# Eleven modulation tiles summed by VectorE instead of TensorE, four of them loaded after the experts, and a gather in four column groups

## The chip, the cores and the metric

The kernel runs on one core of a Trainium2 chip. The time is device time in microseconds (us) of one launch; lower is better. Engines are named as in the profile: PE (TensorE), DVE (VectorE), ACT (ScalarE), POOL (GpSimd) and SP, which here only issues DMA.

## What is computed

Two transformer blocks in float32 for 256 latent tokens and 256 context tokens, width 1024. Each layer's shift, scale and gate rows are a product of an activated condition row with a weight w_ada:

```python
mod_lat = jax.nn.silu(c) @ w_ada[l] + b_ada[l]
sh1, sc1, gt1, sh2, sc2, gt2 = jnp.split(mod_lat[:, None, :], 6, axis=-1)
h_lat = modulate(rmsnorm(x_lat, norm_pre_mix[l]), sh1, sc1)      # h * (1 + scale) + shift
y_lat, y_ctx = token_mixer(h_lat, h_ctx, ...)   # differential attention and a two-way recurrence
x_lat = x_lat + gt1 * rmsnorm(y_lat, norm_post_mix[l])
h_lat = modulate(rmsnorm(x_lat, norm_pre_ffn[l]), sh2, sc2)
f_lat = expert_choice_ffn(h_lat, w_router[l], w_gate[l], w_up[l], w_down[l])  # 16 experts, 32 tokens each
x_lat = x_lat + gt2 * rmsnorm(f_lat, norm_post_ffn[l])
# second block, two layers: latent attention (MLA), then a Fourier mixer
sh_l, sc_l, gt_l = ada_params(silu(c_2), w_ada_2[i], b_ada_2[i])
h_lat = h_lat + gt_l * y_lat
return rms_norm(h_lat, final_g)
```

## The kernel before

The program has a section for each engine, in which every instruction and every wait is written out; the order on an engine is the order of the text. Weights come in tiles of 1024 rows by 512 columns (2 MiB) into `ring`, six slots of that size; in the first part only slots 0 to 3 take them, since 4 and 5 serve as scratch. SP issues the loads in the order of the list `stream` and, before each, waits until the last reader of the slot's former tile (`last_reader`) is through. Since SP issues in order, a load that waits holds back all behind it.

The modulation rows are 24 tiles (`("ada", i)`; 0 to 11 of w_ada, 12 to 23 of w_ada_2). `mod_product(i)` (L886) multiplies one on PE: 8 matmuls in four column groups of 32, 16 passes, since a float32 matmul takes two. ACT copies the result (`take_mod`, L1599). For a shift or scale, PE then turns it into columns (`mod_columns`, L897), and DVE adds the bias (L1990); for a gate, a matmul with a broadcast column spreads it over the partitions (`mod_gate`, L905) and DVE adds it to the gate row `G` (`gate_rows`, L2265). Tiles 18 to 21 (`LATE_MODS`) are different: DVE forms their weighted sum (`late_product`, L2484 and L2487), and PE sums over the partitions only.

The work in order of time: the first four tiles, the forget gates, keys, queries and values out of w_in (L867), among them the eight tiles of `COLUMN_MODS` by `mod_step(k)`, which turns one and multiplies the next. Between them run the levels of the recurrence: DVE makes `distance` (L2107, L2108), ACT the decay (L1644), DVE the products (L2119, L2121), PE the matmuls (L1014). Then differential attention over eight pairs of block and head, n = 0 to 7: scores (L1062), max (L2253), exp (L1716), difference (L2281), transposes (L1090), copy (L1721), value product (L867), and at the end of each n the product of one gate tile. Then the output product, the router (L1194) with a top-k on DVE, and the first gather (L1227), which picks 32 tokens for expert 0 in two column groups of 512 columns.

The 16 experts: `gate_up(e)` (L1262), `down(e)` (L1284), `scatter(e)` (L1296). Each has six tiles of 2 MiB, one for each slot. The first two experts' loads are written out, since parts of the second go to free SBUF (`extra`), the rest runs in a loop. A slot is loaded again as soon as its tile is used. After the experts comes the epilogue: the list `late` with the MLA layer's and the Fourier layer's weights, latent attention over eight heads (scores L1458 and L1464, max L2531, transposes L1488), output product, Fourier layer, its output product (L1551).

## Time and profile before

| | us |
|---|---|
| median of 3 runs | 1079.23 |
| lowest and highest | 1076.66, 1079.52 |
| the profiled execution | 1078.76 |
| its span | 1076.9 |

| engine | busy us | share of the span |
|---|---|---|
| PE | 916.0 | 85% |
| DVE | 334.7 | 31% |
| ACT | 204.0 | 19% |
| POOL | 52.9 | 5% |

The DMA queues moved 310.20 MB, 288 GB/s over the span. A line of the timeline has the start in us, the busy time, engine, source line, operation, what it writes and reads, the number of instructions, and in brackets how long the engine was idle before and what ended that. The chain of waits lists, in order of time, the pieces of the chain that ended last.

### The profile page before, as it was taken

The page shows a single profiled execution, that of the slowest core. Times are in us where ns is not written, and L with a number is a line of the kernel's source. Part 1 is how long each engine was busy: PE and PEld are TensorE (multiplying, and loading weights), DVE is VectorE, ACT ScalarE, POOL GpSimd, SP SyncE. Part 2 cuts the span into 40 slices and gives each one's busy share as a digit, 9 for nine tenths or more (in the row PEclk, how much of TensorE's full clock was granted, in tenths as well). Part 3 has the DMA queues.
Part 4 walks back from the last instruction along what each step waited for, and adds up shares of the span by engine and source line. Part 5 has one row for each costly group of instructions (what it writes and reads, how often), then busy time and mean ns, then how long its engine had stood idle before and what let it go on. Part 6 is the DMA issues. An engine that isn't in the chain of part 4 may idle for free.

```text
span 1076.9 us, 11360 instructions
## 1 busy us (share of the span) xinstructions
PE 916.0 (85%) x4458; PEld 471.7 (44%) x4458; DVE 334.7 (31%) x601; ACT 204.0 (19%) x435; POOL 52.9 (5%) x128
## 2 busy tenths in 40 slices
PE   4999999999999888767777766766678999999997
PEld 2666564674544522222222212222223785644773
DVE  2299615473472331111111101001114365412022
ACT  2123322221452210000000000000004114411121
POOL 0200000000200100000000000000001000000000
PEclk9899999999999989998888888888988999999999
DMA  9973633642699799999999999999999397004200
GB/s 348 344 261 125 227 118 117 234 157 78 234 337 395 276 392 428 423 427 428 428 428 428 428 428 428 428 428 428 428 428 399 141 331 294 1 24 152 79 1 39
DMA packets 66343, 310.20 MB, mean 288 GB/s; under 512 B 2833, under 2 KB 5060, under 8 KB 53636
## 3 DMA queue, kind: packets, MB, share of 16 engines
q1 hardware_dynamic: 63844, 301.04, 70.0%
q0 software_dynamic: 2464, 8.68, 2.4%
q8 instruction: 24, 0.39, 0.1%
q14 instruction: 11, 0.09, 0.0%
HBM read 308.66 MB, written 1.05 MB: 288 GB/s over the span
## 4 chain that ended last, share of the span: by engine, by line
PE 60%; DMA 31%; DVE 3%; ACT 2%; issue 2%; SPq 1%; POOL 0%; POOLq 0%; DVEq 0%; ACTq 0%
PE bank L867 36%; DMA ring<-w_up_dram 27%; PE bank L1262 8%; PE bank L886 3%; PE bank L1551 3%; DMA ring<-w_in_dram 2%; DMA ring<-w_down_dram 2%; PE bank L1458 1%; PE bank L1014 1%; PE bank L1284 1%; PE bank L897 1%; PE bank L876 1%; PE bank L1464 1%; ACT junk L1564 1%; PE bank L1488 1%
## 5 line engine op out<-in xcount | busy, mean ns | idle before, releaser
L1262 PE MATMUL bank<-ring,ilat 128*32 128x512 f32 x972 | 147.4, 757 | 103.3 <-DMA ring<-w_up_dram 102.3
L1262 PEld LDWEIGHTS bank<-ring,ilat 128*32 128x32 f32 x972 | 40.6, 134 | 205.2 <-issue 204.0
L2437 DVE TENSOR_TENSOR state<-state,bank 64x512 f32<-64x512 f32 x16 | 11.0, 690 | 303.1 <-ACT state L1811 303.1
L867 PE MATMUL bank<-ring,hT 128*128 128x512 f32 x224 | 97.1, 593 | 0.0
L867 PE MATMUL bank<-hT,ring 128*128 128x256 f32 (+1 forms) x320 | 88.0, 436 | 4.0 <-DVE hT L2009 2.0
L867 PE MATMUL bank<-ring,kT 128*128 128x512 f32 (+1 forms) x192 | 81.9, 584 | 0.8 <-DVE kT L2549 0.8
L867 PEld LDWEIGHTS bank<-hT,ring 128*128 128x128 f32 x320 | 62.5, 197 | 28.7 <-issue 21.5
L1284 PE MATMUL bank<-ring,ilat 128*32 128x512 f32 x512 | 58.5, 595 | 13.8 <-ACT ilat L1815 12.5
L867 PEld LDWEIGHTS bank<-ring,hT 128*128 128x128 f32 x224 | 42.4, 190 | 52.6 <-issue 51.7
L1296 PE MATMUL bank<-state,ilat 128*128 128x512 f32 x128 | 59.2, 605 | 0.0
L1811 ACT ACTIVATE state<-bank 64x512 f32<-64x512 f32 x16 | 9.5, 592 | 254.5 <-PE bank L1262 254.5
L867 PE MATMUL bank<-kT,ring 128*128 128x256 f32 x256 | 55.7, 379 | 0.0
L867 PEld LDWEIGHTS bank<-ring,kT 128*128 128x128 f32 x192 | 36.1, 190 | 43.1 <-issue 43.1
L867 PEld LDWEIGHTS bank<-kT,ring 128*128 128x128 f32 x256 | 48.6, 190 | 7.4 <-issue 1.0
L886 PE MATMUL bank<-ring,act 128*32 128x512 f32 x320 | 39.2, 613 | 2.4 <-DVE hT L2265 1.5
L1284 PEld LDWEIGHTS bank<-ring,ilat 128*32 128x32 f32 x512 | 15.2, 109 | 45.6 <-issue 38.5
L2441 DVE COPY state<-bank 128x512 f32<-128x512 f32 x16 | 11.1, 692 | 73.5 <-PE bank L1284 73.5
L1296 PEld LDWEIGHTS bank<-state,ilat 128*128 128x128 f32 x128 | 22.9, 189 | 24.9 <-issue 22.5
L1227 PE MATMUL bank<-xres,smat 128*32 128x512 f32 x128 | 32.1, 621 | 0.8 <-DVE smat L2406 0.8
L1551 PE MATMUL bank<-ring,gates 128*128 128x512 f32 x64 | 27.6, 592 | 0.0
L1564 ACT ACTIVATE junk<-xres 128x512 bf16<-128x512 f32 (+1 forms) x18 | 12.2, 679 | 56.9 <-DVE xres L2316 51.7
L1825 ACT ACTIVATE ilat<-bank 128x256 f32<-128x256 f32 x16 | 6.1, 384 | 74.8 <-PE bank L1296 74.8
(368 smaller groups left out, 1051.0 us busy)
## 6 DMA issues: line engine op xcount, KB each, us to landing
ring<-w_down_dram SPq DMA_DIRECT2D x32, 2048.0 KB, 23.7
ring<-w_up_dram SPq DMA_DIRECT2D x29, 2048.0 KB, 23.3
ring<-w_gate_dram SPq DMA_DIRECT2D x29, 2048.0 KB, 18.8
ring<-w_ada_dram SPq DMA_DIRECT2D x24, 2048.0 KB, 9.1
ring<-w_in_dram SPq DMA_DIRECT2D x8, 2048.0 KB, 13.2
ring<-fno_w_in_dram SPq DMA_DIRECT2D x4, 2048.0 KB, 13.0
ring<-w_out_dram SPq DMA_DIRECT2D x2, 2048.0 KB, 9.0
ring<-mla_w_in_dram SPq DMA_DIRECT2D x2, 2048.0 KB, 19.5
```

The lines of the kernel that those rows point to most:

```text
L867: ins = pe.matmul(o, l, r, start=start and i == 0, stop=stop and i == len(terms) - 1)
L876: ins = pe.transpose(o[:, jj * P:(jj + 1) * P], chunk, ident)
L886: ins = pe.matmul(o[32 * q:32 * q + 32, :], act_cols[i // 12][:, j, :], w[:, j, :], start=jj == 0, stop=jj == 1)
L897: ins = pe.matmul(o[:, 2 * jj:2 * jj + 2], chunk, C("sum_columns"), start=True, stop=True)
L1227: ins = pe.matmul(bank[2][32 * g:32 * g + 32, :], x[:, b, :], xr3[:, b, g * TN:(g + 1) * TN], start=b == 0, stop=b == TB - 1)
L1262: ins = pe.matmul(bank[0][32 * t:32 * t + 32, :], xin_cur[:, j, :], x[:, n0:n0 + TN], start=j == 0, stop=j == J - 1)
L1284: ins = pe.matmul(bank[2 + n][32 * q:32 * q + 32, :], hmT[:, q, 32 * c:32 * c + 32], w[4 + c][:, q, n * TN:(n + 1) * TN], start=c == 0, st ...
L1296: ins = pe.matmul(bank[4 + 2 * b + n][:, :], s_cur[:, b * P:(b + 1) * P], yb[n], start=first, stop=last)
L1551: ins = pe.matmul(o[:, :], oT3[:, j, b * P:(b + 1) * P], w[:, j, :], start=j == 0, stop=j == J - 1)
L1564: st.did(act.activation(junk[:, 0:n], src, ACT.Square, scale=float(width) ** -0.5, accum_out=ssq[:, c:c + 1]), sem(signal) if signal else ...
L2437: dve.tensor_tensor(hm, eg, bank[0][64:P, :], ALU.mult).then_inc(freed[0], 1)
L2441: dve.tensor_copy(yb[1], bank[3][:, :]).then_inc(freed[3], 1)
```

## The change

DVE now forms the weighted sums of eleven more tiles with one helper, `weighted_rows`: one multiplication and seven multiply-adds over 128 x 512. These are the four tiles of `FFN_MODS` (6 to 9), three gate tiles (`SUMMED_GATES`: 4, 5, 10), and the last four gate tiles (`LATER_GATES`: 16, 17, 22, 23). The last four leave `stream` for the list `late`; their sums, gate matmuls and row additions stand in the epilogue. Gate tile 11 keeps its PE product. `COLUMN_MODS` has the tiles in another order. SP waits for a sum where it waited for a product. The second expert's tile w_up has three more rows in free SBUF (`extra` number 6), and halves of the first expert's w_down tiles are issued earlier. The first gather and those in the loop work in four column groups of 256 columns. ACT squares the second block's branch before it copies the first block's turned rows.

```diff
-COLUMN_MODS = [6, 7, 8, 9, 12, 13, 14, 15]
+COLUMN_MODS = [12, 13, 6, 7, 8, 9, 14, 15]
-LATER_GATES = GATE_MODS[5:]
+LATER_GATES = GATE_MODS[4:]
+SUMMED_GATES = GATE_MODS[:3]
...
-        for n, i in enumerate(GATE_MODS):
-            if n == 4:
-                tile(("kvctx",), wtile(a["mla_w_in_2"][0], QL, KVL + ROPE))
+        for i in GATE_MODS[:4]:
             mod_tile(i)
+        tile(("kvctx",), wtile(a["mla_w_in_2"][0], QL, KVL + ROPE))
...
                 late_mod(18) + (1,), late_mod(19) + (1,), late_mod(20) + (2,), late_mod(21) + (1,),
+                late_mod(16) + (2,),
                 (("mout", 0), wtile(a["mla_w_out_2"][0], 0), 3),
+                late_mod(17) + (1,),
+                (("mout", 1), wtile(a["mla_w_out_2"][0], TN), 4),
                 (("fin", 0), wtile(a["fno_w_in_2"][0], 0), 2),
-                (("mout", 1), wtile(a["mla_w_out_2"][0], TN), 4),
                 (("fin", 1), wtile(a["fno_w_in_2"][0], TN), 1),
+                late_mod(22) + (5,),
                 (("fin", 2), wtile(a["fno_w_in_2"][0], 2 * TN), 0),
                 (("fin", 3), wtile(a["fno_w_in_2"][0], 3 * TN), 3),
+                late_mod(23) + (5,),
...
+        for name in (("in", 2), ("in", 7)):
+            used_up.remove(name)
+            used_up.insert(used_up.index(("ada", SUMMED_GATES[1])) + 1, name)
...
+            def wait_read(name):
+                if name[0] == "ada" and name[1] in SUMMED_GATES:
+                    sp.wait_ge(sem("gate_sum"), SUMMED_GATES.index(name[1]) + 1)
+                elif name[0] == "ada" and name[1] in FFN_MODS:
+                    sp.wait_ge(sem("column_sum"), FFN_MODS.index(name[1]) + 1)
+                else:
+                    wait_filled(sp, last_reader(name))
...
             extra_tile(0)
             extra_tile(1)
+            sp.wait_ge(sem("scratch_done"), 1)
+            wait_filled(sp, ("gt", SUMMED_GATES[-1]))
+            first_half(EARLY_SLOTS, 2)
+            first_half(EARLY_SLOTS + 1, 0)
+            wait_filled(sp, ("c2T", TB - 1, 1))
+            extra_tile(3)
+            extra_tile(6)
...
-            wait_filled(sp, ("gt", LATER_GATES[-1]))
-            extra_tile(3)
...
-            expert_tile(1, 3, 1)
+            expert_tile(1, 3, 3)
...
                 for b in range(TB):
-                    for g in range(2):
-                        ins = pe.matmul(bank[2][32 * g:32 * g + 32, :], x[:, b, :], xr3[:, b, g * TN:(g + 1) * TN],
+                    for q in range(4):
+                        half, pair_j = divmod(q, 2)
+                        ins = pe.matmul(bank[2][32 * q:32 * q + 32, 0:T], x[:, b, :],
+                                        spread(xr3[:, b, :])[:, half, 2 * pair_j:2 * pair_j + 2, :],
                                         start=b == 0, stop=b == TB - 1)
...
-                if n:
+                if n == len(SUMMED_GATES) + 1:
                     mod_product(GATE_MODS[n - 1])
-            mod_product(GATE_MODS[-1])
...
             for b in range(TB):
                 branch_norm("y", b)
+                if b:
+                    take_turned(0)
                 residual_norm(0, b)
+            take_turned(1)
...
+            def weighted_rows(i, total, signal, j0=0, j1=J):
+                name = ("ada", i)
+                w, col = slot_view(slot_of[name], J, TN), act_cols[i // 12]
+                if j0 == 0:
+                    dve.wait_ge(landed[slot_of[name]], 16 * (turn_of[name] + 1))
+                    step(dve.tensor_scalar(total, w[:, 0, :], col[:, 0, 0:1], None, ALU.mult))
+                for j in range(max(j0, 1), j1):
+                    st.settle()
+                    step(dve.scalar_tensor_tensor(total, w[:, j, :], col[:, j, 0:1], total, ALU.mult, ALU.add),
+                         signal if j == J - 1 else None)
...
+                if i == 0:
+                    column_sum(2)
+                    column_sum(3)
+                if i == 2:
+                    column_sum(4)
                 for k in ks:
                     mod_columns(COLUMN_MODS[k])
+                if i == 2:
+                    column_sum(5)
...
+            gate_sum(0)
+            gate_sum(1)
             dve.wait_ge(sem("rstd_c2"), 1)
             for b in range(TB):
                 step(dve.tensor_scalar(c2[:, b, :], c2[:, b, :], rr[:, b:b + 1], None, ALU.mult), "c2_normed")
+            gate_sum(2)
...
             late_product(3)
+            weighted_rows(LATER_GATES[0], late_gate_sums[0], "late_gate")
...
+                if 1 <= k <= 4:
+                    weighted_rows(LATER_GATES[1], late_gate_sums[1], "late_gate", 2 * k - 2, 2 * k)
...
+            for k in (2, 3):
+                weighted_rows(LATER_GATES[k], late_gate_sums[k], "late_gate")
```

On DVE, after the products of level 0 (L2119 and L2121 of before are L2173 and L2175 of after), the first sums come in front of the column step. Before:

```order
L2119 TENSOR_TENSOR ring<-ring,gates 128x8x64
L2121 TENSOR_TENSOR ring<-ring,qh 128x8x64
L1990 TENSOR_TENSOR modc<-bank,small 128x4
L2107 TENSOR_TENSOR ring<-gates 128x16x32
L2108 TENSOR_TENSOR ring<-gates 128x16x32
L2119 TENSOR_TENSOR ring<-ring,gates 128x16x32
```

and in the changed kernel:

```order
L2173 TENSOR_TENSOR ring<-ring,gates 128x8x64
L2175 TENSOR_TENSOR ring<-ring,qh 128x8x64
L2195 TENSOR_SCALAR vda<-ring,act 128x512
L2198 SCALAR_TENSOR_TENSOR vda<-ring,act,vda 128x512 x7
L2195 TENSOR_SCALAR modr<-ring,act 128x512
L2198 SCALAR_TENSOR_TENSOR modr<-ring,act,modr 128x512 x7
L2044 TENSOR_TENSOR modc<-bank,small 128x4
L2161 TENSOR_TENSOR ring<-gates 128x16x32
```

Two sums, 16 instructions, stand where one column step stood behind the level. On PE, in the attention loop at n = 2 and 3 (transposes of the weights `gates`, scores out of `kT` and `qT`, gate matmul with `const`, value product out of `vda`, context transposes out of `pair`), before:

```order
L1090 MATMUL bank<-const,gates 128x128 x4
L1062 MATMUL bank<-kT,qT 128x512 x2
L905 MATMUL bank<-gates,const 128x512
L867 MATMUL bank<-vda,gates 128x128 x4
L876 MATMUL bank<-const,pair 128x128 x4
L886 MATMUL bank<-ring,act 32x512 x8
L1090 MATMUL bank<-const,gates 128x128 x4
L1062 MATMUL bank<-kT,qT 128x512 x2
L905 MATMUL bank<-modr,const 128x512
```

and in the changed kernel:

```order
L1142 MATMUL bank<-const,gates 128x128 x4
L1114 MATMUL bank<-kT,qT 128x512 x2
L953 MATMUL bank<-pair,const 128x512
L901 MATMUL bank<-vda,gates 128x128 x4
L910 MATMUL bank<-const,pair 128x128 x4
L1142 MATMUL bank<-const,gates 128x128 x4
L1114 MATMUL bank<-kT,qT 128x512 x2
L953 MATMUL bank<-pair,const 128x512
```

The product of a gate tile (L886) between two heads is gone; the gate matmul reads DVE's sum. On DVE in the epilogue, in the heads 1 and 2 of the latent attention (max L2608, scale L2611, reciprocal L2618, normalise L2622), the changed kernel has pieces of a sum between them:

```order
L2608 TENSOR_REDUCE small<-bank 128x2
L2611 TENSOR_SCALAR small<-small 128x2
L2195 TENSOR_SCALAR hT<-ring,act 128x512
L2198 SCALAR_TENSOR_TENSOR hT<-ring,act,hT 128x512
L2618 RECIPROCAL small<-small 128x2
L2622 TENSOR_SCALAR vda<-vda,small 128x512 x2
L2608 TENSOR_REDUCE small<-bank 128x2
L2611 TENSOR_SCALAR small<-small 128x2
L2198 SCALAR_TENSOR_TENSOR hT<-ring,act,hT 128x512 x2
```

Two of the eight instructions of gate tile 17's sum follow each of four maxima; before, the reciprocal came right behind the scale.

## Rows read from the trace of the kernel before

**Rows 1.** The page's 40 slices of 27 us: busy tenths, granted clock, DMA share.

```profile
PE   4999999999999888767777766766678999999997
...
DVE  2299615473472331111111101001114365412022
...
PEclk9899999999999989998888888888988999999999
DMA  9973633642699799999999999999999397004200
```

**Rows 2.** The chain of waits, 150 to 165 us: start us, us, what.

```profile
153.17 1.85 PE bank L886 x16
...
158.83 0.60 ACT state L1655
...
162.95 0.69 DVE ring L2119
```

**Rows 3.** Timeline of DVE, 120 to 275 us, and one late sum (855.11).

```profile
153.28 0.16 DVE L1990 TENSOR_TENSOR modc<-bank,small 128x4 f32<-128x4 f32 x1 [16.90 <-PE bank L897]
...
198.26 0.69 DVE L2119 TENSOR_TENSOR ring<-ring,gates 128x512 f32<-128x512 f32 x1 [11.67 <-ACT ring L1644]
...
248.46 1.29 DVE L2197 TENSOR_TENSOR state<-state,small 128x512 f32<-128x512 f32 x2
256.44 1.42 DVE L2204 TENSOR_SCALAR pair<-pair,small 128x1024 f32<-128x1024 f32 x2 [6.69 <-POOL small L789]
266.76 0.69 DVE L2209 SCALAR_TENSOR_TENSOR ring<-ring,bank 128x512 f32<-128x512 f32 x1 [8.90 <-ACT ring L1701]
...
855.11 5.48 DVE L2487 SCALAR_TENSOR_TENSOR ilat<-ring,act,ilat 128x512 f32<-128x512 f32 x7
```

**Rows 4.** The chain of waits in the attention loop.

```profile
298.43 1.92 PE bank L886 x16
...
308.03 1.24 DVE small L2253
```

**Rows 5.** Timeline of ACT: two exps, and the square behind the turned rows.

```profile
293.52 0.69 ACT L1716 ACTIVATE gates<-bank,small 128x512 f32<-128x512 f32 x1 [2.80 <-DVE small L2256]
...
297.78 0.69 ACT L1716 ACTIVATE gates<-bank,small 128x512 f32<-128x512 f32 x1 [1.84 <-DVE small L2256]
...
361.69 0.59 ACT L1564 ACTIVATE junk<-bank 128x512 bf16<-128x512 f32 x1
```

**Rows 6.** The chain of waits around the first experts.

```profile
379.56 3.63 PE bank L1227 x8
...
385.69 8.77 PE bank L1262 x64
...
394.83 1.84 PE bank L1227 x8
...
427.46 7.05 PE bank L1262 x64
```

**Rows 7.** Timeline of SP: the first load released by expert 0.

```profile
386.97 0.33 SPq L714 DMA_DIRECT2D ring<-w_gate_dram  x1
```

**Rows 8.** Windows: busy us (count) of PE, PEld, DVE, ACT, POOL; PEclk, DMA share, GB/s.

```profile
376.00:380.00 4.00, 1.36 (x8) 0.78 (x10) 2.95 (x9) 2.68 (x7) 0.00 (x0) 0.95 0.99 406
388.00:392.00 4.00, 4.00 (x32) 1.08 (x28) 1.10 (x2) 0.00 (x0) 0.15 (x2) 0.77 0.89 279
400.00:810.00 410.00, 293.32 (x1774) 100.25 (x1770) 43.11 (x73) 28.42 (x58) 16.31 (x53) 0.89 1.01 428
```

**Rows 9.** Timeline of DVE in the epilogue.

```profile
897.81 1.23 DVE L2531 TENSOR_REDUCE small<-bank 128x2 f32<-128x1024 f32 x1 [2.27 <-PE bank L1464]
...
1003.54 0.69 DVE L2581 COPY pair<-bank 128x512 f32<-128x512 f32 x1 [13.04 <-PE bank L867]
```

**Rows 10.** Timeline of PE: gate matmuls, and the second block's output product.

```profile
373.77 1.88 PE L905 MATMUL bank<-pair,const 128*128 128x512 f32 x4
...
946.58 20.84 PE L867 MATMUL bank<-ring,kT 128*128 128x512 f32 x48 [0.82 <-DVE kT L2549]
```

147 lines of the change are left out of this document (89 added, 58 removed).

## The prediction

> **What bounds the kernel now.** I read the page's slices first [rows 1]. They show three regimes. Up to slice 13 (350 us) PE is full and the DMA engines are half idle; in slices 15 to 29 (400 to 810 us) the DMA engines are full and PE is not; after that PE is full again. One window over 400 to 810 us gives the middle its rate: 428 GB/s at a DMA share of 1.01 with PE busy 293 of 410 us [rows 8]. The 16 experts hold 16 x 6 tiles of 2 MiB, 201.3 MB, so a faster PE there gives nothing. What sets the end of that stretch is how early the queue gets going and how many expert bytes are in SBUF by then. The chain of waits says what sets that start: nearly all of it PE work before 350 us, with the products of the modulation tiles (L886) standing in it at 1.85 us each [rows 2].
>
> The profiled execution took 1078.76 us, its span 1076.9; the median of the three runs is 1079.23. I sum against 1078.76 and let the 0.5 us to the median go. A measurement of this kernel can tell about 0.3%, 3.2 us, from no change.
>
> **Part 1, the first 275 us.** Four column tiles (6 to 9) lose their PE product; DVE forms their sums, and PE keeps the column step. By the chain each product is 1.85 us [rows 2]. Three of the four places lie on the path: the two before the S product (in the old order tiles 8 and 9) and the one among the k heads, 5.55 us. The fourth stands between two levels, where the chain leaves PE and goes over the S copy (L1655), a decay and DVE's products (158.83 to 163.6 us and one more) [rows 2]; there it covered a wait, so I give it nothing. The price is on DVE: 8 instructions a tile, of the kind that the late tiles have now, 0.49 us and 7 in 5.48 us, 6.0 us a tile [rows 3]. The first two sums come after level 0, where DVE then sits idle for 16.9 us: 12 us fit. The third and fourth stand around level 2, before the 11.67 us wait for ACT at 198.26 [rows 3]; both fit with about 3 us left. If that cover were gone each sum would cost up to its 6.0 us. SP now waits for a sum instead of a product before it loads w_in tiles 1 and 0; sum 6 is done about 142 us and tile w_in 1 is wanted at 162, so the load (about 5 us at 428 GB/s) is hidden. Sum: 5.55 us.
>
> **Part 2, attention.** The sums of gate tiles 4, 5 and 10 stand after the scaled states, where DVE idles 6.69 and 8.90 us and is busy 1.4 us between them [rows 3]. Tile 4's sum starts at 249.8 in the old times (where the states end [rows 3]), 5's at 255.7, the context norm follows at 261.7 and 10's sum ends at 269.1; the gate of w_in 7 starts then and not at 266.76, and its second half, at 273.6, is met. So: 18 us of DVE, hidden, margin 3 us. Tile 10 is loaded only after sum 4 (255.8), so it lands near 261, in time.
> From the eight gate products in the attention loop seven go, and one gate matmul pair: 7 x 1.92 us [rows 4] and 0.94 us (half of the 1.88 us that four such passes take [rows 10]), 14.4 us of PE. Not all of it comes back. What comes next is the ring max (DVE, 1.24 + 0.17 us), exp (ACT, 1.6 us), difference (DVE, 1.2 us), max: two exps that nothing else held up stand 4.26 us apart, 293.52 and 297.78 [rows 5], and the max is already on the chain [rows 4]. I walked the eight heads through with that ring and the other pieces at their own durations: exp 5 at 301.9, exp 6 at 306.9 (behind the squares and the root of block 0), exp 7 at 313.9 (PE has to do the one product left, then the scores), last value product at 322.0. The output product starts there and not at 331.8. Taken: 9.8 us; bounds 5 us (a lost overlap in two of the heads) and 14.4 us (PE alone).
>
> **Part 3, the router and the new entry.** ACT now squares branch 1 before it copies the turned rows of block 0. It began at 361.69, after waiting for a transpose [rows 5]; its first half can go some 7 us earlier and the second at 360.6, so the residual of block 1 is ready 1.8 us sooner and the logits start 1.7 us sooner. The first gather goes from two column groups to four with half the columns in each: 3.63 us [rows 6] becomes 1.8: where PE has its full clock, two groups take 1.84 us for 8 passes of 512 columns [rows 6], and four groups 1.92 us for 16 [rows 4], twice the rate. That its reading is now strided is shown nowhere, so it could give nothing (bound 0). Copying 256 columns rather than 512 and two transposes rather than four give 0.5 more. Sum: 1.7 + 2.35 = 4.05 us.
> So the first expert's product, at 385.69 [rows 6], starts 5.55 + 9.8 + 4.05 = 19.4 us earlier.
>
> **Part 4, the expert stretch.** Before the first expert frees its first rows (386.97 us [rows 7]), SP has issued 19.4 MB of expert weights; after, 20.4 MB, since rows 1 to 3 of the second expert's w_up tile go to free SBUF. The other halves and extras are only issued earlier. Four gate tiles, 8.4 MB, are out of the way. That they are does not itself shorten anything: DMA is idle before 387 us in the new order (I get the last tile landed by about 369, counted without part 1's shift, with first rows at 373), so the entry follows PE. From there 1.05 MB less has to come: 1.05 / 0.428 = 2.4 us. The queue must run dry before the entry and pays a new start; now it only dips (279 GB/s in 388 to 392 us [rows 8], 1.4 us lost), so I add nothing for one and take 0.7 us off for both. The last weights land 19.4 + 2.4 - 0.7 = 21.1 us earlier. The order of the loop is as it was.
>
> **Part 5, the epilogue.** It is PE's, and it takes four sums, 24 us of DVE, four gate matmuls and four row additions of 0.7 us. Sum 16 is in front of the value copies and the first max: DVE's max stands at 897.81 after 2.27 us of idle [rows 9], and 6.0 us in front move it to 900.5, so that PE's first transposes, which began near 904.1, come near 904.8: 0.7 us. Sum 17 is cut in four pieces of 1.6 us between the heads, which have about 3 us of slack each; I allow 0.5 us at the last. Sums 22 and 23 come after the last turned block, before a copy that waits 13.04 us [rows 9]: the copies that they delay are wanted at 1031. The first two gate matmuls take 1.9 us, 0.8 of which PE waited anyway before 946.58 [rows 10]: 1.1 us. The last two stand between spectrum and output product with no wait now: 1.8 us. Sum: +4.1 us; bounds 2.9 (matmuls alone) and 10 (sum 16 in full, and two heads late).
>
> **Sum.** 1078.8 - 21.1 + 4.1 = 1061.8; I forecast **1061.5 us**.
>
> **Against a rule.** The granted clock fell from 1.00 to 0.95 and below after a stretch of 4 us in which PE was busy 1.36 us [rows 8], and with it the first gather and the first expert's product were slow, 8.77 us for 64 passes [rows 6]. A thinner attention loop offers PE more such pauses. The Trainium skill says the same in TensorE: Matmul & The Clock Gate, section HAM oscillation — how this bites in real kernels: a matmul stretch broken up by waits falls back to the half clock, and every piece starts cold. The rows speak for such a fall only after the router's pause; the attention loop now runs at 1.00 though it waits for DVE and ACT.
>
> **Rivals.**
> 1. *The clock falls in the thinned loop.* PE would be busy some 26 of 34 us there, in gaps under 3 us. If it fell to its 1.2 GHz level at the entry to the output product, it would lose about what one fall loses now, by [rows 6]: 1.8 us on the gather (3.63 against 1.84) and 1.7 us on the product (8.77 against 7.05), once or twice. Time 1061.8 + 3.5 to 7 = 1067. For it: the row of 1.36 us. Against: gaps are shorter. Chance 0.12.
> 2. *The loop is PE's after all*, and all 14.4 us come back: 1057. For it: PE is busy 9 tenths there. Against: 4.26 us between unhindered exps. With better cover in the epilogue 1055.5. Chance 0.15.
> 3. *DVE and ACT take the gain in attention*: only 5 us, and half of part 3: 1078.8 - 21.1 + 4.8 + 2 + 4.1 = 1068.6. Chance 0.10.
> 4. *The epilogue's sums lie on the path* (slower). If DVE were the engine that PE waits for through the whole epilogue, the sums would cost 24 us, the row additions 2.8 and the matmuls 3.7: 1078.8 - 21.1 + 30.5 = 1088. It decides from 21 us on the path. Against: DVE is at 1 to 4 tenths there, with 20 us of PE between the turned blocks and the spectra. Chance 0.04.
> 5. *The sums don't move the entry*: a sum on the path at each of the three places of parts 1 and 2 (5 to 6 us each) and no strided gain eat up what the products gave: about 1077. Chance 0.04.
>
> **How the numbers follow.** My forecast with its own spread (1057.5 to 1065.5) has 0.55. Together with rivals 1, 2 and 3 the cases run from 1055 to 1069; outside lie rivals 4 and 5 and the tails. Range 1054.5 to 1069. Faster by over 0.3%: 0.92 (forecast, rivals 1 to 3); within: 0.04; slower: 0.04.
>
> **What would show it.** In the profile after: the gate product L886 should have 9 tiles, not 20; DVE should show 15 sums of 6.0 us, not 4; the second S product at about 151; the last value product of attention near 316.5 (322.0 less 5.55); the first expert product near 366.3, with 1.8 us of gather; a gap in the DMA before it; the stretch at 428 GB/s ending 21 us earlier; the epilogue from last expert product to end 4 us longer. It would be wrong if a bank or a slot that I took as free is held by a sum, if exps stand over 5 us apart in the thinned loop, or if the DMA rate is not 428 GB/s.

## The result, and the profile after

The changed kernel takes 1067.85 us (median of 6 runs, 1066.82 to 1071.75), the kernel before 1078.23 (6 runs, 1076.00 to 1079.52). The ratio is 0.9903, with a 95% interval of 0.9890 to 0.9916. The prediction was 1061.5 with a range of 1054.5 to 1069: the sign and the range held, but the gain is 10.4 us where 17 were forecast. The profiled execution took 1067.25 us, its span is 1065.4, 11.5 us below the span of before. The page has these rows against [rows 1] (a slice is now 26.6 us):

```profile
DVE  2199766679562511000000000000004484623232
...
PEclk9899999999999999888889888888889998999999
DMA  9973462644478799999999999999997785343300
```

DVE has more work in most of slices 4 to 10 and again from slice 31 on (counted from 0, as in the prediction), and the full DMA stretch ends earlier. So the change does what it says. The question is where 5.5 us of the expected gain stayed. Reading the same events in both traces, stage by stage, gives the answer in one table. "Shift" is the time of after less the time of before at the end of the stage; the stage's own share is in the third column.

| up to | shift | this stage | forecast |
|---|---|---|---|
| the S copy (ACT, 158.83 in [rows 2], now 152.57) | -6.3 | -6.3 | -5.55 |
| the second gate tanh of w_in 7 (269.2) | -3.8 | +2.5 | 0 |
| output product starts (331.8, now 320.4) | -11.4 | -7.6 | -9.8 |
| first expert product ([rows 6], now 370.47) | -15.2 | -3.8 | -4.05 |
| last w_up tile lands (809.7, now 789.9) | -19.7 | -4.5 | -1.7 |
| end | -11.5 | +8.2 | +4.1 |

Of the 6.3 us in the first line 0.7 were there before anything changed (PE's first gate product starts at 26.83 and not at 27.50), so 5.6 are part 1's.

**Level 1.** The chain of waits of after, 152 to 176 us (start us, us, what), and under it two windows (busy us of PE, PEld, DVE, ACT, POOL; PEclk, DMA share, GB/s):

```profile
152.57 0.60 ACT state L1707
...
158.02 3.78 PE bank L1066 x16
161.80 14.62 PE bank L901 x32
```

```profile
156.00:160.00 4.00, 2.06 (x10) 1.98 (x10) 3.76 (x8) 1.06 (x1) 0.00 (x0) 0.58 0.97 352
160.00:164.00 4.00, 4.00 (x13) 2.73 (x13) 3.96 (x7) 1.50 (x2) 0.00 (x0) 0.57 0.01 4
```

PE waits 1.95 us in front of level 1's products (L1066), in the place where the fourth column product stood. Then the granted clock is 0.58 and 0.57 over eight microseconds: in the records PE is at the 1.2 GHz level. The 16 passes take 3.78 us where they took 2.05 before, and the first two k heads 14.62 instead of 13.74.

**Attention.** The same chain at the last heads:

```profile
310.26 1.45 ACT gates L1766 x4
311.70 1.40 ACT ring L1787 x4
...
313.64 2.08 PE bank L901 x8
315.71 1.61 PE bank L910 x8
...
319.41 4.59 PE bank L901 x16
```

The eighth head's exp stands at 310.26, within 0.2 us of my walk through the ring (313.9 less the 3.8 us by which the loop starts earlier). The seventh head's value product waits 2.22 us for ACT, which does that exp and a context copy first, and stands at 313.64. Behind the wait PE's passes are slow: 2.08 us for eight of them against 1.05 to 1.16 in the earlier heads, at a clock of 0.71 and 0.87 over 312 to 320 us. The last value product comes at 319.41 and not at 316.5.

**DVE's sums** lie where they were expected, and hide. Timeline of DVE: the second column sum, the first and the third gate sum, the gates of w_in 7, against [rows 3]:

```profile
138.52 5.47 DVE L2198 SCALAR_TENSOR_TENSOR modr<-ring,act,modr 128x512 f32<-128x512 f32 x7
...
246.40 5.48 DVE L2198 SCALAR_TENSOR_TENSOR pair<-ring,act,pair 128x512 f32<-128x512 f32 x7
...
260.10 5.47 DVE L2198 SCALAR_TENSOR_TENSOR ring<-ring,act 128x512 f32<-128x512 f32 x7
...
269.84 0.69 DVE L2293 SCALAR_TENSOR_TENSOR ring<-ring,bank 128x512 f32<-128x512 f32 x1 [2.95 <-ACT ring L1751]
```

The second gate still waits 2.95 us for ACT: the three sums before it cost the path nothing.

**The entry.** Chain and windows, against [rows 6] and [rows 8]:

```profile
354.39 1.20 PE bank L1244 x16
...
366.43 2.06 PE bank L1276 x16
...
370.47 7.07 PE bank L1311 x64
```

```profile
368.00:372.00 4.00, 2.41 (x22) 0.75 (x22) 2.82 (x6) 0.00 (x0) 0.02 (x1) 0.97 0.01 4
372.00:376.00 4.00, 4.00 (x40) 1.17 (x36) 0.08 (x1) 0.00 (x0) 0.64 (x3) 1.00 0.77 205
...
400.00:780.00 380.00, 265.79 (x1700) 88.47 (x1692) 35.02 (x68) 26.38 (x54) 15.06 (x49) 0.88 1.01 428
```

The queue does run dry (4 GB/s) before the first expert frees its rows, and the long stretch again runs at 428 GB/s. PE's timeline has the last w_up wait, `L1311`, at 789.93, where before it stood at 809.68.

**The epilogue.** Timelines of PE and DVE around the first scores of the MLA part, against [rows 9]:

```profile
875.23 1.88 PE L1508 MATMUL bank<-ring,pair 128*128 128x512 f32 x4
...
880.93 3.75 PE L1508 MATMUL bank<-ring,pair 128*128 128x512 f32 x4 [2.76 <-DVE gates L2600]
884.61 2.08 PE L1514 MATMUL bank<-qT,vda 64*128 64x512 f32 x4
...
890.42 1.89 PE L1538 MATMUL bank<-const,smat 128*128 128x128 f32 x8
```

```profile
874.70 5.47 DVE L2198 SCALAR_TENSOR_TENSOR hT<-ring,act,hT 128x512 f32<-128x512 f32 x7
880.10 1.28 DVE L2600 COPY gates<-bank 128x512 f32<-128x512 f32 x2
881.29 1.21 DVE L2608 TENSOR_REDUCE small<-bank 128x2 f32<-128x1024 f32 x1
```

Sum 16 ends at 880.1. Only then does DVE copy the values (L2600), and the second scores need the bank that this copy frees. PE waits 2.76 us for it, and the passes behind the wait are slow: the second scores take 3.75 us against 1.98 before. From the first scores to the first transposes (L1538) it is 15.19 us, where the kernel before needs 9.44 (894.64 to 904.08). Of these 5.75 us the wait is 2.76, and the slow passes are nearly all the rest.

### The profile page after: what moved, and what is told of

The parts are those of the page before. It is cut to its first block, busy times and chain, and to the rows that moved or that the text cites. A ratio compares the mean times of both kernels' runs of the same rounds, so it can differ in the third digit from the quotient of the medians.

```text
span 1065.4 us, 11266 instructions
## 1 busy us (share of the span) xinstructions
PE 893.4 (84%) x4378; PEld 467.4 (44%) x4378; DVE 390.1 (37%) x689; ACT 197.7 (19%) x424; POOL 53.2 (5%) x128
## 3 DMA queue, kind: packets, MB, share of 16 engines
HBM read 308.66 MB, written 1.05 MB: 291 GB/s over the span
## 4 chain that ended last, share of the span: by engine, by line
PE 58%; DMA 31%; DVE 5%; ACT 2%; issue 2%; SPq 1%; POOL 0%; POOLq 0%; DVEq 0%; ACTq 0%
PE bank L901 36%; DMA ring<-w_up_dram 28%; PE bank L1311 8%; PE bank L1605 3%; DMA ring<-w_in_dram 2%; DMA ring<-w_down_dram 2%; PE bank L1508 1%; PE bank L1066 1%; PE bank L920 1%; PE bank L1333 1%; PE bank L1514 1%; PE bank L1538 1%; ACT junk L1618 1%; PE bank L910 1%; DVE small L2337 1%
## 5 line engine op out<-in xcount | busy, mean ns | idle before, releaser
L1311 PE MATMUL bank<-ring,ilat 128*32 128x512 f32 x964 | 146.7, 762 | 106.3 <-DMA ring<-w_up_dram 105.3
L1311 PEld LDWEIGHTS bank<-ring,ilat 128*32 128x32 f32 x964 | 40.3, 135 | 209.3 <-issue 208.1
L1276 PE MATMUL bank<-xres,smat 128*32 128x256 f32 x256 | 32.1, 628 | 0.8 <-DVE smat L2492 0.8
L2198 DVE SCALAR_TENSOR_TENSOR hT<-ring,act,hT 128x512 f32<-128x512 f32 x28 | 21.1, 752 | 1.0
L1508 PE MATMUL bank<-ring,pair 128*128 128x512 f32 x32 | 17.8, 687 | 2.8 <-DVE gates L2600 2.8
## 6 DMA issues: line engine op xcount, KB each, us to landing
ring<-fno_w_in_dram SPq DMA_DIRECT2D x4, 2048.0 KB, 10.4
```

The costliest lines, as they stand in the source:

```text
L1276: ins = pe.matmul(bank[2][32 * q:32 * q + 32, 0:T], x[:, b, :], spread(xr3[:, b, :])[:, half, 2 * pair_j:2 * pair_j + 2, :], start=b == 0, ...
L1311: ins = pe.matmul(bank[0][32 * t:32 * t + 32, :], xin_cur[:, j, :], x[:, n0:n0 + TN], start=j == 0, stop=j == J - 1)
L1508: pe.matmul(o[i][:, :], qnT[:, 2 * m + i, b * P:(b + 1) * P], knT[:, 2 * m + i, :], start=True, stop=False)
L2198: step(dve.scalar_tensor_tensor(total, w[:, j, :], col[:, j, 0:1], total, ALU.mult, ALU.add), signal if j == J - 1 else None)
```

## Experiments

Three theories were open. The *clock* theory: where work was taken off PE, the wait that it had covered is now a pause, and the pause costs twice, since the passes behind it run at half the clock. The *bank* theory: sum 16 costs by the bank that it keeps from PE, not by DVE's time. The rival to both is DVE itself: its 15 sums delay what PE waits for, wherever they stand.

The kernel before ran beside each batch of experiments, with medians of 1078.23, 1079.57, 1079.30 and 1080.16 us. So medians of different batches can differ by up to 2 us without a reason in the kernels; the ratio to the kernel before (0.9903 for the changed kernel) and the distances between events within one trace are the safer figures.

### Spreading sums 16 and 17

```diff
             late_product(3)
-            weighted_rows(LATER_GATES[0], late_gate_sums[0], "late_gate")
...
-                if 1 <= k <= 4:
-                    weighted_rows(LATER_GATES[1], late_gate_sums[1], "late_gate", 2 * k - 2, 2 * k)
+                n = k // 4
+                weighted_rows(LATER_GATES[n], late_gate_sums[n], "late_gate", 2 * (k % 4), 2 * (k % 4) + 2)
```

> The changed kernel with the sums of gate tiles 16 and 17 both cut into pieces of two rows, one piece in each of the eight steps of the MLA head loop; no instruction more or less. In the changed kernel sum 16 stands in front of DVE's two value copies, the second scores wait for the bank that such a copy frees (880.93, 2.76 us of PE idle), and the granted clock is 0.53 to 0.81 over 880 to 896 us; L1538 is 6.1 us later than forecast. If the place of the sum is the cause (bank and clock together), no PE idle of over 1 us before the second scores, clock 1.00 over that stretch, and the end comes 5 to 6 us earlier: span near 1060, time near 1061.7. If DVE's time itself is what PE pays (24 us of sums on a DVE that PE waits for), the six microseconds only move into the head loop and the time stays at 1067.

Measured: 1064.45 us (4 runs, 1063.24 to 1065.75), ratio 0.9860 (0.9840 to 0.9879). Same DVE work, 3.4 us faster than the changed kernel: DVE's time is not what PE pays. The idle time before the second scores is gone, and from the first scores to the end it is 186.45 us instead of 190.17. But the expected full clock did not come, so the gain is short of 5 to 6 us. Timeline of PE, with its windows:

```profile
885.10 2.95 PE L1525 MATMUL bank<-const,qh 128*128 128x2 f32 x16
887.91 1.95 PE L1538 MATMUL bank<-const,smat 128*128 128x128 f32 x8
889.65 3.35 PE L1508 MATMUL bank<-ring,pair 128*128 128x512 f32 x4
```

```profile
884.00:888.00 4.00, 4.00 (x29) 4.00 (x29) 3.00 (x8) 2.31 (x8) 0.00 (x0) 0.72 1.05 387
888.00:892.00 4.00, 4.00 (x12) 2.66 (x12) 0.34 (x2) 1.20 (x2) 0.00 (x0) 0.50 0.29 107
```

PE counts as busy without a break here, and the clock falls all the same, while it works through matmuls of two columns.

### Sum 16 behind the value copies

```diff
             late_product(3)
-            weighted_rows(LATER_GATES[0], late_gate_sums[0], "late_gate")
             for b in range(TB):
                 o = wait_filled(dve, ("v2", b, 1))
                 frees(st, dve.tensor_copy(v2[:, b, TN:2 * TN], o[:, :]), ("v2", b, 1))
+            weighted_rows(LATER_GATES[0], late_gate_sums[0], "late_gate")
```

> The changed kernel with sum 16 in one piece as before, but behind the two value copies instead of in front of them (still in front of the first max). It tells the bank from DVE's time. If the held bank is what costs (the step that the forecast missed), the second scores start without the 2.76 us of idle, the first max comes about 6 us late against 2.3 us of slack there, and the time is some 3 to 4.7 us below the changed kernel's: 1062.5 to 1064. If DVE's 6 us in front of the first max is the whole cost, nothing changes: 1067, within 1 us.

Measured: 1067.1 us (one run), by the time alone the second case. The trace says otherwise about the place itself. The second scores start without a wait, and PE's wait moves to the first transposes:

```profile
889.42 1.94 PE L1538 MATMUL bank<-const,smat 128*128 128x128 f32 x8 [2.45 <-DVE smat L2622]
```

From the first scores to these transposes it is 12.02 us: 3.2 less than with the sum in front (15.19), 2.6 more than before (9.44). So freeing the bank early takes 3.2 of the 5.75 us away here, and 2.6 remain as a wait for DVE: max, exp and normalising behind the sum have no slack for it. How large the first part is depends on how deep the clock falls: in the traces of four other kernels below with sum 16 in front of the copies (level filled, column products back, gate products back, rows undone) the 15.19 us are 13.84 to 14.13. The 3.2 us do not show in the time: the start was 0.5 us later, the last expert's products behind the last weights took 6.29 and 5.24 us against 6.10 and 3.64 in the changed kernel, and the third scores behind the transposes were slower too (3.62 against 2.79). One run's total is too coarse for this step; the place in the trace is less so.

### Two idle products in front of level 1

```diff
+            def idle_products(name, n=2):
+                o = pe_take(pe, name)
+                for _ in range(n):
+                    pe.matmul(o[:, :], C("ones"), const[:, 0:TN], start=True, stop=True)
...
             mod_step(4)
+            idle_products(("lv", 1, 0), 2)
             level(1)
```

> The changed kernel with two more PE products of 512 columns (1.9 us, their result is overwritten and never read) in front of level 1's products, where PE stands idle for 1.95 us at 156.1. In the changed kernel the granted clock is 0.58 and 0.57 over 156 to 164 us, level 1's 16 passes take 3.78 us and the k heads 14.62. If the idle stretch is what takes the clock away (the product removed there had hidden it), the clock stays at 1.00, the 16 passes take 2.05 and the k heads 13.74, and everything from the k heads on comes 2.6 us earlier although PE does more: time near 1064.6. If the slow passes come from anything else (their data, a DMA burst, DVE at the same banks), the products stay slow and the time is 1067 to 1069.

Measured: 1059.97 us (one run), more than the 2.6 us expected. Timeline of PE and windows:

```profile
155.75 1.96 PE L963 MATMUL bank<-const 128*128 128x512 f32 x4
157.84 2.05 PE L1071 MATMUL bank<-ring 128*128 128x128 f32 x16
159.72 13.90 PE L901 MATMUL bank<-hT,ring 128*128 128x512 f32 x32
```

```profile
156.00:160.00 4.00, 3.88 (x21) 2.49 (x21) 3.76 (x7) 1.06 (x1) 0.00 (x0) 1.00 0.95 347
...
312.00:316.00 4.00, 2.54 (x21) 2.09 (x20) 1.36 (x4) 1.19 (x2) 0.00 (x0) 1.00 0.00 0
```

Work that nobody reads, in place of a pause, and the 16 passes are back at 2.05 us: level 2 starts 36.75 us after level 0 instead of 39.37. This is the clock theory. The rest was not expected: the clock does not fall in the attention loop either, though the seventh head still waits 2.23 us there. From level 0 to the output product it is 163.77 us instead of 168.03, 4.3 us less. The other 2.8 us came behind the first expert product (1.4 in the expert stretch and its tail, 1.3 in the epilogue), where nothing was edited.

### Two idle products in the attention loop

```diff
                     mod_gate(GATE_MODS[n - 2])
+                if n == 6:
+                    idle_products(("y", 0, 0), 2)
```

> The changed kernel with two more PE products of 512 columns (1.9 us, result never read) before the value product of the seventh head, where PE stands idle for 2.22 us before 313.64. In the changed kernel the clock is 0.71 over 312 to 316 and 0.87 over 316 to 320, and L901 x8 takes 2.08 us, L910 x8 1.81 there. If the idle stretch takes the clock away, the passes are back at 1.16 and 1.2 us, the clock at 1.00, and the output product comes 1.5 to 2.3 us earlier: time 1065 to 1065.7. If the thin loop is slow for another reason, or the gain is eaten by DVE and ACT, the output product starts at 320.4 as now or later.

Measured in the loop as the clock theory has it: value product and turns are back at full speed, and from level 0 to the output product it is 166.63 us, 1.4 less than in the changed kernel.

```profile
312.25 1.88 PE L963 MATMUL bank<-const 128*128 128x512 f32 x4
314.64 1.16 PE L901 MATMUL bank<-vda,gates 128*128 128x128 f32 x8 [0.51 <-ACT gates L1778]
315.63 1.04 PE L910 MATMUL bank<-const,pair 128*128 128x128 f32 x8
```

The time, 1068.48 us (one run), is not lower: level 0 came 0.8 us later and the expert stretch took 421.2 us from the first product to the last w_up tile, against 418.8 to 419.8 in the changed kernel and the three above. Again a gain of 1.4 us at its place is less than what one run varies by elsewhere.

### Part 1 undone

```diff
-            if k < len(COLUMN_MODS) and COLUMN_MODS[k] not in FFN_MODS:
+            if k < len(COLUMN_MODS):
                 pclaim(("mod", COLUMN_MODS[k]))
...
-                if i == 0:
-                    column_sum(2)
-                    column_sum(3)
```

> The changed kernel with part 1 undone: the four column tiles 6 to 9 are PE products again (and ACT copies), DVE forms no sum for them; everything else is as changed. Theory (three products of 1.85 us were on the path, and the fourth, between levels 0 and 1, kept the granted clock up): the second S product comes 3.7 us later, one more product stands among the k heads, but level 1 and the k heads are back at the full clock (2.05 and 13.74 us), so that the rotary and cross part comes 5.55 - 2.6 = 3 us later and the time is 1070 to 1071 (1068.5 if attention also escapes its fall of the clock, as it did in the kernel with filled level 1). Rival (the slow clock has nothing to do with the removed product): 5.55 us later, time 1073.

Measured: 1068.74 us (4 runs, 1066.43 to 1071.71), ratio 0.9908 (0.9882 to 0.9933). Taking four products of 1.85 us off PE is worth 0.9 us in the medians, which the intervals don't tell from nothing; in the traces, from PE's first gate product to the output product, it is 1.9 us (295.50 against 293.57). The trace has the first case with its bracket: the second S product is later as it should be, level 1 takes 2.05 us and the k heads run at full clock, and the attention loop keeps its clock:

```profile
161.81 2.05 PE L1061 MATMUL bank<-ring 128*128 128x128 f32 x16
163.70 13.90 PE L899 MATMUL bank<-hT,ring 128*128 128x512 f32 x32
```

### Gate tiles 4, 5 and 10 back on PE

```diff
-SUMMED_GATES = GATE_MODS[:3]
+SUMMED_GATES = []
...
-                if n == len(SUMMED_GATES) + 1:
+                if 1 <= n <= 4:
                     mod_product(GATE_MODS[n - 1])
```

> The changed kernel with gate tiles 4, 5 and 10 back as PE products in the attention loop (and ACT copies), no sums for them on DVE; the last four gate tiles stay in the epilogue. It parts the seven products that left the loop into three (here) and four. Theory (the loop is a ring of max, exp and difference, in which a product is partly hidden; the thin last heads lose the clock): the stretch from the first scores to the output product grows by 3 x 1.92 + part of the gate pair, less what is hidden, 4 to 5 us, and without a fall of the clock at 312 to 320 us by 1.5 to 2 us less: time 1069.5 to 1072. Rival (loop is PE's alone): 3 x 1.92 + 1.9 = 7.7 us, time 1075. Rival (the ring of ACT and DVE alone): nothing, 1067.

Measured: 1071.91 us (4 runs, 1071.24 to 1072.02), ratio 0.9926 (0.9909 to 0.9942), inside the first case. From level 0 to the output product it is 171.23 us, 3.2 more than in the changed kernel, and 1.8 more come between output product and logits, where the clock is 0.50 over 320 to 328 us. So the three sums bring 4.1 us in the medians, 2.5 by the ratios (whose intervals overlap), and 5.0 us in the traces up to the logits, a part of which is this kernel's deeper fall of the clock. The loop is partly PE's and partly the ring's, as the walk had it. That the fuller loop would keep its clock was wrong: it fell with the products back in it.

### The preloaded rows undone

```diff
-                 (2, 2, JH, tmpb), (3, 0, 1, G[0]), (3, 1, 3, hT[:, 2 * D:4 * D])]
+                 (2, 2, JH, tmpb), (3, 0, 1, G[0])]
...
-            expert_tile(1, 3, 3)
+            expert_tile(1, 3, 1)
```

> The changed kernel without the preload of rows 1 to 3 of the second expert's w_up tile: 1.05 MB more has to come after the first expert product. Theory (bytes at 428 GB/s): time from the first expert product to the landing of the last w_up tile grows by 2.4 us from 419.5 (the kernels so far had 418.8 to 421.2), time 1069.5. Rival (the entry and not the bytes sets the end of the stretch): no change, 1067.

Measured: 1069.45 us (4 runs, 1065.87 to 1070.84), ratio 0.9900 (0.9873 to 0.9927). The landing of the last w_up tile, seen as the end of PE's wait,

```profile
793.65 4.91 PE L1310 MATMUL bank<-ring,ilat 128*32 128x512 f32 x32 [6.15 <-DMA ring<-w_up_dram]
```

comes 422.09 us after the first expert product; it was 419.46 in the changed kernel. That is 2.6 us for 1.05 MB, where 2.4 were expected. The distance alone would not show it, since kernels with the same loads have 418.60 to 421.22 us. The bytes do: summed over windows, 178.8 MB come in this stretch and 177.8 in the changed kernel, 1.0 MB or 2.3 us at 428 GB/s. The time does not tell it from nothing (ratio 0.9900 beside 0.9903).

### The gather in two groups

```diff
-                    for q in range(4):
-                        half, pair_j = divmod(q, 2)
-                        ins = pe.matmul(bank[2][32 * q:32 * q + 32, 0:T], x[:, b, :],
-                                        spread(xr3[:, b, :])[:, half, 2 * pair_j:2 * pair_j + 2, :],
+                    for g in range(2):
+                        ins = pe.matmul(bank[2][32 * g:32 * g + 32, :], x[:, b, :], xr3[:, b, g * TN:(g + 1) * TN],
```

> The changed kernel with the gather in two column groups of 512 columns, the row copy of 512 columns and four turns of 64, as in the kernel before. Theory: only the first gather is on a path: it takes 3.6 us instead of 2.06, copy and turns 0.5 us more, so the first expert product stands 2.1 us later behind the logits (16.1 us after them now): time 1069. Rival (the other fifteen gathers too are on a path, because PE is kept from the weights): time 1071 or more. Rival (the stretch is DMA's and has slack at its entry): no change.

Measured: 1073.62 us (4 runs, 1072.31 to 1074.41), ratio 0.9943 (0.9925 to 0.9961), 5.8 us above the changed kernel's median (4.3 by the ratios) where the theory had 2. Timeline of PE:

```profile
366.94 3.63 PE L1275 MATMUL bank<-xres,smat 128*32 128x512 f32 x8 [0.83 <-DVE smat L2491]
...
373.13 9.97 PE L1310 MATMUL bank<-ring,ilat 128*32 128x512 f32 x64 [0.97 <-DVE ilat L2506]
...
383.40 1.91 PE L1275 MATMUL bank<-xres,smat 128*32 128x512 f32 x8
```

The first product is 18.24 us behind the logits instead of 16.08, the 2.1 us expected. But the product behind it also takes 9.97 us instead of 7.07, at a clock of 0.50 to 0.62 over 368 to 380 us: the first expert's rows come free later (SP's third pair of loads is issued 6.6 us after the product's start and not 3.9). The last w_up tile lands 421.41 us after the product's start, 2.0 more, but a kernel with the fast product had 421.22, so that this part is not shown to come from the gather. Behind that tile another 1.5 us are lost, where nothing was edited. The other fifteen gathers are not to blame; in the loop they take 1.91 us, and 2.00 in the form with four groups, which is no gain from four groups at all; more of that below.

### The edits that paid, together

The edits of the first and the third experiment:

```diff
+            idle_products(("lv", 1, 0), 2)
             level(1)
...
+                n = k // 4
+                weighted_rows(LATER_GATES[n], late_gate_sums[n], "late_gate", 2 * (k % 4), 2 * (k % 4) + 2)
```

> The two edits that paid in a profile, together on the changed kernel: sums 16 and 17 in eight pieces of two rows in the MLA head loop, and two more PE products of 512 columns (result never read) in front of level 1's products. If the causes are separate (a held bank with its clock in the epilogue: 3.7 us from the first scores to the end; the clock at level 1, and with it in attention: 4.3 us from level 0 to the output product) they add up: 1067.85 - 3.7 - 4.3 = 1059.9, and 1058.5 with the shorter tail that the filled kernel had. If the single run with the filled level (1059.97) was a lucky one, the median is 1062 to 1064.

Measured: **1057.40 us** (5 runs, 1056.26 to 1058.18), ratio 0.9795 (0.9781 to 0.9810). This beats both kernels: 22.8 us below the kernel before beside it, and 10.4 below the changed kernel's median (11.6 by the ratios). The two gains add up, and 1 to 2.5 us more came. From level 0 to the output product it is 163.78 us, as with the level filled; from the first scores to the end it is 183.16 and not 186.45, because in this kernel the clock does not fall in the epilogue either:

```profile
878.89 1.93 PE L1531 MATMUL bank<-const,qh 128*128 128x2 f32 x16
880.67 1.07 PE L1544 MATMUL bank<-const,smat 128*128 128x128 f32 x8
881.58 1.88 PE L1514 MATMUL bank<-ring,pair 128*128 128x512 f32 x4
```

These are the same instructions, with no wait of over 1 us before them either, as in the kernel with the spread sums alone (2.95, 1.95, 3.35 us), 6 us earlier in the program's run. Nothing in that part differs between the two programs, and yet 3.3 us lie between them.

### Parting the two-column matmuls

```diff
+            late_columns((0, 1))
...
                     fills(ins, ("pT", n))
+                    if n == 0:
+                        fills(late_columns((2, 3)), ("late_columns",))
```

> The kernel before this one in the list (spread sums, filled level 1) with the 16 two-column matmul pairs of the late column tiles parted: half of them before the first transposes, half between the first head's and the second's. It asks whether idle time alone takes the clock away: with the sums spread PE has no idle of over 1 us there, and yet the clock is 0.72 and 0.50 over 884 to 892 us and the first transposes, the third scores and half of the columns take 5.3 us more at the half clock than they would at the full one (2.95, 1.95 and 3.35 us against 1.93, 1.05 and 1.88: 3.4 us). If a run of matmuls of two columns counts as a pause, parting it keeps most of the clock: 2 to 3 us off, time near 1057.5. If only idle time counts, the parting adds about 0.9 us of idle and the time is 1060 or a little more.

Measured: 1060.28 us (5 runs, 1057.35 to 1064.70), ratio 0.9817 (0.9795 to 0.9839). That is 2.9 us above the kernel with all of them in one piece, with intervals that overlap; the profiled run was the slowest of the five. In it the clock fell after all, right there (0.80, 0.50, 0.50 over 880 to 892 us). The expectation went by the kernel with the spread sums alone, and of its two figures for the slow passes the 3.4 us is the right sum. The kernel with two edits keeps its clock with the 16 pairs in one piece, so a run of two-column matmuls by itself does not always take it. Parting it brings a wait of 0.67 us and wins nothing.

### More idle products

```diff
                 for i in pair_of:
                     mod_columns(i)
+                idle_products(("xT", 1, 0, 0) if half else ("z", 0, 0))
...
             context_latent(1, (1,))
+            idle_products(("kvcT",))
```

> The kernel with the parted columns, and three more pairs of idle PE products of 512 columns (1.9 us each): two in the first 45 us, where PE waits 1.98 us at 24.5 and 2.03 us at 40.9 before the first gate's products (which then take 8.71 and 5.38 us for 32 and 16 passes of 256 columns, against 3.62 us for 16 at the full clock), and one in the router, where PE waits 2.80 us for the context rows, with the first gather at 2.02 us behind it. If a pause before them is what slows these passes, the first gate comes 1.5 + 1.7 us earlier and the gather 1 us: the time falls by 3 to 4 us, to about 1054. If the start is bound by the loads (DMA is at 0.9 to 1 there), only the router's 1 us comes through, and if the fillers delay their successors the time rises by up to 2 us.

Measured: 1062.48 us (5 runs, 1059.18 to 1067.33), ratio 0.9847 (0.9820 to 0.9874). At the start the fillers do what was expected, against the kernel with two edits: the first gate's 32 passes take 7.14 us and not 10.10, the next 16 take 3.69 and not 6.39, and level 0 comes 2.7 us earlier than with two edits (151.54 against 154.20). All of it is lost in attention:

```profile
310.21 1.50 PE L901 MATMUL bank<-vda,gates 128*128 128x128 f32 x8 [2.23 <-ACT gates L1785]
311.50 1.92 PE L910 MATMUL bank<-const,pair 128*128 128x128 f32 x8
```

The loop has the same pauses as in the kernel with two edits (2.23, 0.78, 0.69 us), but here the clock is 0.86, 0.50, 0.50 and 0.86 over 308 to 324 us, so that the output product starts at 317.83, 0.15 us before that kernel's. The output product itself is slow at its start, so that the logits come 1.5 us later than there. The router's filler brought nothing: from the logits to the first expert product it is 16.22 us with it and 16.13 without.

### When the same pause costs, and when not

The profiles together, clock at three places where the program has a pause or thin work:

| kernel | level 1 | attention, 7th head | MLA, first heads |
|---|---|---|---|
| before | full (product there) | full | 0.66 |
| changed | 0.57 | 0.71 | 0.53 |
| sums spread | 0.50 | 0.60 | 0.50 |
| sum behind | 0.50 | 0.77 | 0.50 |
| level filled | full | full | 0.57 |
| attention filled | 0.50 | full (filled) | 0.50 |
| column products back | full | full | 0.69 |
| gate products back | 0.50 | 0.50 | 0.57 |
| rows undone | 0.50 | 0.70 | 0.59 |
| two groups | 0.50 | 0.77 | 0.50 |
| two edits | full | full | full |
| columns parted | full | full | 0.50 |
| more fillers | full | 0.50 | 0.57 |

(The lowest window of 4 us around the place; full is 1.00.) At level 1 the column is clean: seven kernels with the pause all fell, six with work in it all kept the clock. In the attention loop the last two heads have the same pauses (2.23, 0.78 and 0.69 us) in all kernels but two, the one before and the filled one. Of these eleven seven fell and four did not, and all six that had fallen at level 1 fell here too. In the MLA part every kernel but one fell, some with no pause of over 1 us. So the pause of 1.95 us took the clock each time and the one of 2.23 us in some kernels, filling either kept it, and whether a given pause does take it also depends on something that the order of the instructions does not show. That a fall at level 1 brings on the one in attention is not shown: the kernel with more fillers fell in attention alone.

## Why the prediction was right, and where it was wrong

The direction and 10.4 of the 17 us came: the sums on DVE hide in the first 350 us, and PE's time up to the first expert product is what the change shortens. That the time lies in the range is partly luck. The first product is 4.2 us late and the epilogue 4.1 us too long, and the stretch between them is 2.8 us better for a reason that I did not have. That rival 1 names nearly the measured time (1067) is luck as well: the clock fell, but elsewhere, and the largest miss has another cause.

**Part 1** took 5.6 us off the path before the S copy, as forecast, and the four sums hid. The step that failed is the sentence on the fourth product: it "covered a wait, so I give it nothing". Its removal was worth less than nothing. The wait that it had covered became a pause of 1.95 us with the slow passes behind it, +2.6 us, shown by filling it. With the fall in attention that came in every kernel that had lost the clock here (unless that pause was filled), the whole of part 1 is worth 0.9 us in the medians and 1.9 in the traces (part 1 undone).

**Part 2**: sums and ring were right to 0.2 us up to the eighth exp (310.26). Then came rival 1, which had a chance of 0.12: the clock falls in the thinned loop. I had placed and priced it at the output product (3.5 to 7 us in all, 1067); it came a head and a half earlier. Against the walk, shifted by what the loop really started with (322.0 less 3.8, 318.2), the last value product at 319.41 is 1.2 us late, and filling the pause brought 1.4. The other 1.0 us of the 2.2 is a slip of mine in the last step: the walk gave the start of the last value product, and I let the output product start at that same time, though the value product takes 1.0 us first (319.41 to 320.40). The argument against it ("gaps are shorter" than the router's) was the error: a gap of 2.22 us was enough. Yet the loop alone isn't the cause: it kept its clock in four kernels that had not lost it at level 1. The Trainium skill says in TensorE: Matmul & The Clock Gate, section HAM oscillation — how this bites in real kernels, that a matmul stretch broken up by waits falls back to the half clock and each piece starts cold. The trace agrees at level 1, with 3.78 us against 2.05; the waits in the page's example are 3 to 5 us long, and here one of 1.95 us was enough. In attention the runs agree in seven kernels and not in four, so the rule alone does not decide. Still, I should have asked that rule about every place where a product left PE, not about the loop alone.

**Part 3**: router order 1.8 us (forecast 1.7), right. The entry behind the logits 2.0 us (forecast 2.35), right in size but not in reason. I had read two rates, two groups 1.84 us and four groups 1.92 for twice the passes, and concluded that four groups with half the columns halve whatever the two groups take. At the full clock the strided gather takes 2.00 us, no less than the two groups' 1.84 to 1.91. It wins 1.6 us only since the first gather falls where the clock is down: the two groups then take 3.63, the strided four still 2.06.

**Part 4**: 4.5 us and not 1.7, and the terms that failed are the bytes and the restart. Two windows have it, from the first expert product to the landing of the last w_up tile, in the kernel before and in the changed one:

```profile
385.69:809.68 423.99, 306.84 (x1865) 104.17 (x1866) 47.85 (x81) 29.67 (x61) 18.12 (x60) 0.89 1.01 426
370.47:789.93 419.46, 299.71 (x1955) 99.75 (x1956) 40.28 (x78) 29.58 (x61) 18.12 (x60) 0.88 1.00 424
```

That is 180.6 MB before and 177.8 after (each window's us times its GB/s), 2.8 MB less, or 6.4 us at 428 GB/s. The preloaded rows are 1.0 MB of it (2.3 us, forecast 2.4). The other 1.7 MB, 4 us, were loads that the kernel before still had under way when its product started (406 GB/s at 376 to 380 us [rows 8]); in the changed kernel all had landed and the queue stood at 4 GB/s. I had counted bytes issued, not bytes landed. Against this stands the restart, for which I took 0.7 us off: over the first 16 us behind the product's start the DMA moved 374 GB/s before and 312 after, which is 2.1 and 4.2 us lost against 428. So the dry queue did cost about 2 us, and 6.4 less 2 gives the 4.5. That the first product is faster now (7.07 against 8.77 us) brings the loads that it releases forward, but no experiment parts it from the rest.

**Part 5**, the largest miss: 8.2 us and not 4.1. The last w_up tile to the first scores is unchanged (+0.3), from the first scores to the first transposes it is +5.8, from there to the end +2.2. The last number holds sum 17 and four gate matmuls (two pairs of 1.7 us) and is less than the 3.4 forecast, partly since the kernel before has a fall of the clock there itself (3.33 us for the third scores). The first transposes are the step that failed: "6.0 us in front move it to 900.5", and from there 0.7 us. It followed sum 16 to DVE's max and stopped. Behind the same sum on DVE stood the value copy, and behind that on PE the bank of the second scores. Even without the bank 0.7 us was too little: with the sum behind the copies the delay of the max alone costs 2.6 us. The prediction named this as what would make it wrong ("a bank or a slot that I took as free is held by a sum"); reading what DVE has queued between the sum and the max would have shown it. Spread over the heads, the same work leaves 10.46 us from the first scores to the transposes, of which another fall of the clock is 1.0; with both edits it is 9.43, as in the kernel before.

In sum: the first product 4.2 us later than forecast (2.5 at level 1, 2.2 in attention and 0.2 at the entry, less the 0.7 of an earlier start), the stretch behind it 2.8 better, the epilogue 4.1 worse: 5.5 us, the difference of the spans' 11.5 and the forecast 17.

**What stays open.** Why the same pause takes the clock in one kernel and not in another: the spread sums alone and with the filled level have the same MLA code, and only the first fell. The Trainium skill, same page, section What's actually happening, notes that the count of slow matmuls differs from run to run of one kernel. That fits the scatter here (the kernel with parted columns ran from 1057.35 to 1064.70), but no run here shows its cause. So 2 to 4 us of the distance between the best kernel and its neighbours may be luck of position, though its own five runs lie within 1.9 us. Each kernel has one profile, so how often a kernel with a given order keeps its clock at a given place is not known.

## What to carry to other kernels

Work taken off PE where it covered a wait is not free: look in the trace for the pause left behind and for slow passes after it (pauses of 1.95 and 2.23 us had them here), and try putting something into it, even products that nobody reads. Do it pause by pause, with a measurement each time: three more fillers won 2.7 us at the start of the program and lost them again in attention. Before moving a long piece of work ahead of others on an engine, list every instruction queued behind it up to the next wait, and for each one the bank or slot that it frees, not only the one on the path. Where several edits of 1 to 3 us are tested, compare positions within a stage; the total of one run varies by more than that for reasons elsewhere.

## What was not expected of the hardware

A wait of 1.95 us on PE, with matmuls of two columns ahead of it, was followed in all seven kernels that have it by a fall of the clock, in the changed kernel to 0.58 (the 1.2 GHz level for the most part) over the next eight microseconds; 1.9 us of idle products in its place kept it at 1.00. The clock fell also with no wait over 1 us, at 0.72 and 0.50 over 884 to 892 us, in a stretch in which PE counts as busy throughout.

A moving operand read with a stride of four elements is not faster in four column groups: 16 passes of 256 such columns take 2.00 us, while 16 passes of 512 adjacent ones take 1.92 (L920). The time is nearly the same where the clock was 0.61 (2.06 us). So there something other than the clock sets the rate; what it is was not tested. In this kernel the form helps only where the clock is down.
